# Other places modulo 256 bytes for the moving rows of five feed-forwards, and one wait on TensorE

## What is computed

```python
for l in range(DEPTH):
    h = h + 0.5 * swiglu(rms_norm(h, ffn1_norm[l]), ffn1_w_gu[l], ffn1_w_down[l])
    ...
    h = h + 0.5 * swiglu(rms_norm(h, ffn2_norm[l]), ffn2_w_gu[l], ffn2_w_down[l])
return rms_norm(h, final_norm)[:, N_META:]
```

## Time and profile before

| | |
|---|---|
| median of 3 executions | 2347.76 us (2346.85 to 2353.99) |
| the profiled execution | 2351.31 us |
| its span, first to last instruction | 2349.5 us |
| matmuls | 18270, busy 2234.5 us |
| VectorE, ScalarE, GpSimd busy | 1400.5, 1161.1, 558.9 us |
| mean granted clock of TensorE | 0.98 |
| HBM read | 377.80 MB, 162 GB/s over the span |

### The profile page before, as it was taken

One profiled execution on the slowest core, in us unless ns is written; L12 is line 12 of the kernel. 1 busy time (PEld: TensorE's weight loads), 2 busy tenths in 40 slices (PEclk: granted clock), 3 DMA queues, 4 the chain that ended last, 5 costly groups with the idle time before them and its releaser, 6 DMA issues.

```text
span 2349.5 us, 49109 instructions
## 1 busy us (share of the span) xinstructions
PE 2234.5 (95%) x18270; PEld 2193.3 (93%) x18270; DVE 1400.5 (60%) x1966; ACT 1161.1 (49%) x1752; POOL 558.9 (24%) x589
## 2 busy tenths in 40 slices
PE   7999999999999999899999999985999999988998
PEld 7999988999999999889999899985999999988998
DVE  6555866655555556856565565486664656466553
ACT  5444544454445436344454455466554545446553
POOL 4322000232213311000342243024431123112420
PEclk9999999999999999999999999998999999999999
DMA  6554433455545645233466466443565556543663
GB/s 212 184 186 158 145 99 113 131 168 172 183 164 172 199 150 178 86 96 109 161 199 201 137 203 217 161 147 96 161 206 188 184 177 190 192 144 97 195 202 116
DMA packets 99259, 380.47 MB, mean 162 GB/s; under 512 B 10912, under 2 KB 13088, under 8 KB 99017
## 3 DMA queue, kind: packets, MB, share of 16 engines
q1 hardware_dynamic: 99144, 378.91, 50.2%
HBM read 377.80 MB, written 3.16 MB: 162 GB/s over the span
## 4 chain that ended last, share of the span: by engine, by line
PE 84%; DVE 6%; ACT 4%; issue 3%; DVEq 2%; POOL 1%; POOLq 1%; DMA 0%; ACTq 0%; SPq 0%
PE bank L607 25%; PE bank L609 25%; PE bank L608 25%; ACT whi L1021 2%; DVE wlo L1425 2%; PE bank L667 1%; PE bank L668 1%; PE bank L669 1%; PE bank L884 1%; PE bank L625 1%; POOLq L1987 1%; PE bank L794 1%; PE bank L873 0%; DVE cv L1761 0%; PE bank L863 0%
## 5 line engine op out<-in xcount | busy, mean ns | idle before, releaser
L1425 DVE TENSOR_TENSOR wlo<-raw,whi 128x1024 fp32r<-128x1024 f32 (+1 forms) x660 | 871.9, 1333 | 520.4 <-ACT whi L1021 518.2
L1021 ACT ACTIVATE whi<-raw 128x1024 fp32r<-128x1024 f32 (+1 forms) x660 | 729.1, 1117 | 428.6 <-PE bank L609 395.2
L607 PE MATMUL bank<-x_tokens_hi,wlo 128*128 128x256 f32 x1784 | 496.3, 278 | 6.2 <-DVE z L1777 3.9
L608 PE MATMUL bank<-x_tokens_lo,whi 128*128 128x256 f32 x1784 | 494.5, 277 | 0.0
L609 PE MATMUL bank<-x_tokens_hi,whi 128*128 128x256 f32 x1784 | 494.5, 277 | 0.0
L607 PEld LDWEIGHTS bank<-x_tokens_hi,wlo 128*128 128x128 f32 x1784 | 334.9, 188 | 8.5 <-issue 3.8
L608 PEld LDWEIGHTS bank<-x_tokens_lo,whi 128*128 128x128 f32 x1784 | 336.5, 189 | 0.0
L609 PEld LDWEIGHTS bank<-x_tokens_hi,whi 128*128 128x128 f32 x1784 | 335.1, 188 | 0.0
L2007 POOL TENSOR_TENSOR z<-sil,z 128x256 f32<-128x256 f32 (+1 forms) x176 | 178.0, 1012 | 561.0 <-DVE z L1469 411.7
L609 PE MATMUL bank<-hid_tokens_hi,whi 128*128 128x256 f32 x880 | 243.8, 277 | 0.0
L607 PE MATMUL bank<-hid_tokens_hi,wlo 128*128 128x256 f32 x880 | 243.8, 277 | 0.0
(11 more groups left out here) (384 smaller groups left out, 4950.1 us busy)
## 6 DMA issues: line engine op xcount, KB each, us to landing
raw<-ffn_gu SPq DMA_DIRECT2D x352, 512.0 KB, 4.1
raw<-ffn_down SPq DMA_DIRECT2D x128, 704.0 KB, 4.1
raw<-mix SPq DMA_DIRECT2D x120, 512.0 KB, 3.5
raw<-rec SPq DMA_DIRECT2D x28, 512.0 KB, 3.8
raw<-kv SPq DMA_DIRECT2D x16, 512.0 KB, 4.2
raw<-att SPq DMA_DIRECT2D x16, 512.0 KB, 3.6
bias_rows<-rows SPq DMA_DIRECT2D x8, 256.0 KB, 4.3
bias<-bias_rows SPq DMA_DIRECT2D x1, 1536.0 KB, 8.6
```

The source lines that it names most:

```text
L607: pe.matmul(out, wlo[:, slot, w], xh(i), start=(i == 0), stop=False)
L608: pe.matmul(out, whi[:, slot, w], xl(i), start=False, stop=False)
L1021: act.activation(whi[:, k, 0:cols], raw[:, k, 0:cols], ACT.Copy).then_inc(hi_made, 1)
L1425: dve.tensor_tensor(wlo[:, k, 0:cols], raw[:, k, 0:cols], whi[:, k, 0:cols].bitcast(F32), ALU.subtract).then_inc(lo_made, 1)
```

## The change

The second feed-forward of the first layer gets remainder 64 instead of 192. Each of the four feed-forwards of the second block gets pairs of arrays of its own over the same memory, both for its input rows and for its hidden rows, with remainders 32 (F4), 96 (F5), 160 (F6) and 224 (F7) instead of 64. REC, KV and ATT stay at 64. `top[0]` and `hid_end` move down by 128 bytes and `ebase` up by 64, and with them what lies behind. And on TensorE, a feed-forward without a norm of its own, which is F6 alone, waits after its sixth tile (t = 5) until that tile is done.

```diff
@@ -277,7 +277,7 @@
         raw = at("raw", [P, RING, CH11], F32)
         whi = at("whi", [P, RING, CH11], F32R)
         wlo = at("wlo", [P, RING, CH11], F32R)
-        LINE, SHIFT, BACK_SHIFT, ROW = 256, 64, 192, T + 48
+        LINE, SHIFT, ROW = 256, 64, T + 48
 
         def pair_at(name, count, first, cols):
 
@@ -290,9 +290,10 @@
         xbase = line_after(top[0])
         x_tokens = pair_at("x_tokens", KD, xbase + SHIFT, SEQ)
         X = {0: pair_at("x_first", KD, xbase + SHIFT, ROW), 1: pair_at("x_mixer", KD, xbase + SHIFT, ROW),
-             2: pair_at("x_second", KD, xbase + BACK_SHIFT, ROW), "last": x_tokens, "F4": x_tokens, "REC": x_tokens,
-             "F5": x_tokens, "F6": x_tokens, "ATT": x_tokens, "F7": x_tokens}
-        top[0] = xbase + BACK_SHIFT + 2 * KD * ROW * 4
+             2: pair_at("x_second", KD, xbase + SHIFT, ROW), "last": x_tokens, "REC": x_tokens, "ATT": x_tokens}
+        PLACES = {"F4": 32, "F5": 96, "F6": 160, "F7": 224}
+        X.update({s: pair_at("x_" + s, KD, xbase + place, SEQ) for s, place in PLACES.items()})
+        top[0] = xbase + SHIFT + 2 * KD * ROW * 4
         h = at("h", [P, KD, T], F32)
         consts = at("consts", [P, N_CONST], F32)
         masks = at("masks", [P, MASKED_LEVELS, P], U8)
@@ -315,10 +316,10 @@
         idle, warm = at("idle", [P, 1], F32), at("warm", [P, 1], F32)
         hbase = line_after(top[0])
         hid_tokens = pair_at("hid_tokens", KF, hbase + SHIFT, SEQ)
-        HID = {0: pair_at("hid_first", KF, hbase + SHIFT, ROW), 2: pair_at("hid_second", KF, hbase + BACK_SHIFT, ROW),
-               "last": hid_tokens, "F4": hid_tokens, "F5": hid_tokens,
-               "F6": hid_tokens, "F7": hid_tokens}
-        hid_end, ebase = hbase + BACK_SHIFT + 2 * KF * ROW * 4, hbase + BACK_SHIFT + 2 * KF * SEQ * 4
+        HID = {0: pair_at("hid_first", KF, hbase + SHIFT, ROW), 2: pair_at("hid_second", KF, hbase + SHIFT, ROW),
+               "last": hid_tokens}
+        HID.update({s: pair_at("hid_" + s, KF, hbase + place, SEQ) for s, place in PLACES.items()})
+        hid_end, ebase = hbase + SHIFT + 2 * KF * ROW * 4, hbase + LINE + 2 * KF * SEQ * 4
 
 
         H, E = [hbase], [ebase]
@@ -706,8 +707,11 @@
                     k8_tile(q + t // RING, t % RING, j + 4 if t == 7 else None, early_bank(t), X[s], c)
                     if t == (4 if c else 3) and main_norm:
                         input_norm(x, n, c)()
-                    if t == (5 if c else 4) and main_norm:
-                        norm_back_drained(n, c)
+                    if t == (5 if c else 4):
+                        if main_norm:
+                            norm_back_drained(n, c)
+                        else:
+                            pe.wait_ge(tile_done, j + t + 1)
                 with pe.Fori(2, FFN_GU_QUADS) as b:
                     for k in range(RING):
                         k8_tile(b + q, k, b * RING + j + k - 3, k, X[s], c)
```

## The result

| | before | after |
|---|---|---|
| median | 2352.94 us (6 runs, 2346.85 to 2360.6) | 2372.17 us (6 runs, 2366.8 to 2374.96) |
| profiled execution | 2351.31 us | 2374.96 us |
| its span | 2349.5 us | 2373.2 us |

The change makes the kernel slower: ratio 1.0072, 95% interval 1.0048 to 1.0095, or 19.2 us on the medians.

What follows compares the result with a forecast made beforehand. TensorE's matmuls were taken as the bound, a feed-forward's time being products times pitch. Terms -5.3 + 5.3 + 5.3 + 3.5 + 0.3 + 10.1 = +19.2 us gave a median of 2367.0 us, range 2336 to 2395.

Steps and rivals of the forecast that it cites:

- First layer's second feed-forward: Rows from 192 to 64: 1584 products at 123.3 instead of 126.7 ns, 5.3 us less.
- F4 at 32: Second block: pitch 116.7 instead of 113.3 ns, the mean of neighbours 0 and 64, +5.3 us.
- F5 at 96: Second block: pitch 116.7 ns, the mean of neighbours 64 and 128, +5.3 us.
- F6 at 160: Second block: pitch 120.0 instead of 117.8 ns, between slow neighbours 128 and 192, +3.5 us.
- F7 at 224: Second block: pitch 120.0 ns, between slow neighbours; products behind and before the norm's sum together +10.1 us.
- The wait: F6, after its sixth tile: PE waits for that tile's last product; only the cost counted, +0.3 us.
- Rival 5: Wait in F6 leaves the rhythm as it is; alters nothing at the forecast's place values; chance 0.08.
- the rotating rows: 256-column rows taking 0, 64, 128, 192 in turn: 118.3 ns, from which 0 and 192 were put at 120.0 each.
- the first (all as good as 64): F4 to F7: 32-byte places run at 113.3 ns once drained; -11.4 us, 2336.4; chance 0.14.
- The third (all at 120.0): F4 to F7 all at the known slow pitch, 120.0 ns; +29.8 us, 2377.6; chance 0.16.
- The fourth (dearer than 120): F4 to F7: odd multiples of 32 dearer than any known place, 126.7 ns; +72.2 us, 2420.0; chance 0.10.
- The second, that the place doesn't matter: Feed-forwards: only rhythm counts, so F6 gains 6.1 us and nothing else changes; 2341.7 us; chance 0.06.

Runs made afterwards that it cites:

- e1_all64: The change with F4 to F7 back at 64 and without the wait in F6; 2363.35 us median, 1.0031 times the kernel before.

## Why the prediction was right

The direction and the mechanism held: TensorE stays the limit, and each stage costs its products times the pitch of its place. The size held in part by luck: 2367.0 was forecast, as +19.2 us against a median of 2347.8; measured are 2372.2, +19.2 us on the medians of this comparison and +23.7 between the profiles. That the medians' difference agrees to a tenth is chance, since one stage's rhythm is worth 6 us. Term by term, by the profile:

- *First layer's second feed-forward, -5.3:* 123.3 ns, as forecast, and -5.3 us; run by itself it gives 0.9971.
- *F4 at 32, +5.3:* 118.8 ns and not 116.7, +8.6. *F5 at 96, +5.3:* 118.3, +7.9. The mean of the two neighbours was too kind: 32 is no better than 0, and 96 has a quarter of the way from 128's 120.0 to 113.3. Only 64 itself stands out.
- *F6 at 160, +3.5:* 116.7 and not 120.0, -1.7. Here the neighbours were too dear, since 192 costs 117.8 at rest and not 120.0. *F7 at 224, +10.1:* 120.0, +10.1. Its neighbours were wrong in the same way, and it came out right by luck (taken directly, +9.2).
- *The wait, +0.3:* 0.31 us, and no gain at 160. At 64 a stop can turn the rhythm, but the kernel isn't faster on the whole by it. Rival 5, that the wait leaves the rhythm as it is, came true at 160, where it alters nothing in the sum.

The four places together: forecast 5.3 + 5.3 + 3.5 + 10.1 = 24.2, measured 24.9. The terms' errors cancelled. The mean over the four, 118.45, is near the 118.3 of the rotating rows, on which all four terms together rest, but that is luck too: at rest the four places that those rows take average 117.5 with 64 fast. Two errors of about the same size met, 0 and 192 put too dear and 32 and 96 too cheap.

What I left out, first: that 64 itself isn't one state. I had seen both rhythms and three feed-forwards turning fast, and read the drain as something that keeps the fast one. In the profiles of the twelve kernels that have such stages (rows at 64, weights at 128, 256 columns, a drained norm or the wait) there are 39 of them: 6 are slow behind the drain, 4 more turn slow at tile t = 10, 29 stay at 113.3. (F6 without drain or wait turned slow there once more, in the kernel with the middle moved.) The one in the profile after is the +6.0 us that stands between the forecast and the profiles' difference. Between profiles these draws are nearly all of the spread: over the seven kernels of the experiments with all stages at 64 the feed-forwards together take 1505.5 to 1523.7 us, and all the rest of the kernel 830.0 to 834.5. That the 5 us by which the median of before moved, and most of the 13 to 25 us that its executions span in a session, are such draws too is argued and not shown: only profiled executions show the rhythm, and the timed ones of the first two all-64 kernels were all slower than their profiled one.

Second: that the splits stay hidden. The prediction counted ACT and DVE as never in the way in a feed-forward. In a fast one TensorE waits for VectorE's low part at t = 10, for 0.01 to 0.04 us with a drained norm and 0.13 to 0.17 us in an F6 without one. That is little by itself, but all five turns away from the drains and norm sums happened at this wait.

On the rivals: the first (all as good as 64) needs a mean below 114, it was 118.45. The third (all at 120.0) was 1.5 ns too dear in the mean, and its 2377.6 us lies as near to the measured 2372.2 as the forecast's 2367.0; it is the pitches that decide against it, of which only 224 has 120.0. The fourth (dearer than 120) found nothing, 120.0 is the worst of all eight places. The second, that the place doesn't matter, is excluded by the run with moved weights, where rows at an unchanged remainder went from 123.3 to 126.6 ns. The Trainium skill, SBUF — State Buffer, section Who interferes with whom, has the moving operand and the weights on independent read ports. If that were all, the place of the one against the other would cost nothing; these runs don't agree with that for float32r products. The 109.2 ns that the prediction took from the Trainium skill, TensorE: Matmul & The Clock Gate, section Back-to-back issue gap, is given there for a single matmul by itself; the section says that in a stream of weight loads and matmuls both set the spacing, and the pairs here took 113.3 ns at best.

## What to carry to other kernels

In a stream of matmuls whose weights are exchanged every time, read the pitch from starts before anything else, and try the rows' place against the weights' modulo 256 bytes: over the eight multiples of 32 it was worth up to 6% of every product here (113.3 to 120.0 ns). Compare places by their rows in one profile, several in one kernel; compare kernels only over many executions, since one place can have two rhythms and a profile shows one draw. Before a pause is put down to the chip, look whether the program waits there and when what it waits for was ready: here it was VectorE's low part, 0.1 us ahead. A change of layout moves everything behind it: move one array and keep the room of the old one, or its effect can't be told from that of the rest; so done, the first layer's part alone beats both kernels (2349.4 us, 0.9971; with the end of the layout moved too 2352.3 us in another session, 0.9958, the intervals overlap).

## What the runs showed of the hardware that was not expected

- With 256 columns and the weights at 128, the pitch by place is: 0 118.7; 32 118.8 or 117.3; 64 113.3 or 117.8; 96 118.3; 128 120.0; 160 116.7 or 117.8; 192 117.8; 224 120.0 ns. With 272 columns: 64 123.3, 192 126.7. It goes with the place against the weights' and not with the rows' own: with the weights 128 bytes further on, six stages had the pitches of places 128 bytes away.
- The rhythm can be turned by four small matmuls, by a full drain, or by a wait that holds a product back by as little as 7 ns (e1_all64's F5), the drain in both directions; by the wait at t = 10 only to the slow one, in 5 of the 34 stages at 64 that met it. Between such events it never changed in these profiles, over 1344 products at a time.
- A weight load that waited for VectorE's low part started 0.12 to 0.13 us after the end of the instruction that made it, in all 35 stages that show this wait.
- TensorE's granted clock was 0.99 to 1.00 in the windows of the feed-forwards shown, before and after, so neither place nor rhythm is the clock's doing.
